# Two transformer blocks on one core: a shorter inverse root, narrower weight tiles, a finer start and moved weight splits

## The reference

```python
def rms_norm(x, g, eps):
    return x * rsqrt(mean(x * x) + eps) * g

# second block
proj = rms_norm(h, attn_pre_norm) @ w_in       # w_in: 1024 x 2072
(q_n, k_c, v_c, k_s, v_s, k_w, v_w, g_n, q_w, k_sw, v_sw) = split(proj, IN_SPLITS)
# k_sw: 2 heads x 64 = 128 columns; v_sw: 128 columns; g_n: 8 heads x 3 = 24 columns
k_c, v_c -> compress -> 15 compressed keys and values
mixed = concat([rms_norm(o_nsa), rms_norm(o_swa)]) @ w_out
h = h + rms_norm(mixed, attn_post_norm)
u = causal_dwconv(rms_norm(h, ffn_pre_norm) @ w_up)
out = h + rms_norm((gelu(gate) * up) @ w_down, ffn_post_norm)
```

## Time and profile before

| | us |
|---|---|
| three runs | 1249.72, 1247.06, 1248.22 (median 1248.22) |
| the profiled execution | 1248.38, of which the span of its instructions is 1246.5 |

### The profile page before, as it was taken

How to read it: one execution, slowest core, us unless ns; L and a number is a source line. 1 busy time by engine, 2 the same in 40 slices (tenths; PEclk the granted TensorE clock), 3 DMA queues, 4 the chain that set the end, 5 groups by cost and what they waited for, 6 DMA issues and landing times.

```text
span 1246.5 us, 24096 instructions
## 1 busy us (share of the span) xinstructions
PE 1182.5 (95%) x9150; PEld 1125.3 (90%) x9150; DVE 892.2 (72%) x1520; ACT 610.0 (49%) x1070; POOL 67.6 (5%) x56
## 2 busy tenths in 40 slices
PE   9999999999999999998999999999978898999997
PEld 8988898999999999778989999999966587999997
DVE  7999876676666587556758666556886757999854
ACT  5764644544445444344445444444455654666642
POOL 1576000000000000000000000000000000000000
PEclk9999999999999999998999999999988898999999
DMA  7453442455455556214524555556544113454563
GB/s 274 170 201 136 136 169 101 140 170 197 169 190 182 198 177 217 68 69 152 186 82 143 199 180 191 172 200 211 185 168 137 35 35 100 159 197 170 187 211 107
DMA packets 32232, 198.55 MB, mean 159 GB/s; under 512 B 3744, under 2 KB 6944, under 8 KB 9248
## 3 DMA queue, kind: packets, MB, share of 16 engines
q1 hardware_dynamic: 30240, 194.14, 45.1%
q10 hardware_dynamic: 1920, 3.41, 0.8%
HBM read 194.12 MB, written 1.05 MB: 157 GB/s over the span
## 4 chain that ended last, share of the span: by engine, by line
PE 80%; DVE 12%; ACT 4%; issue 3%; DMA 1%; DVEq 0%; ACTq 0%; SPq 0%
PE acc L495 20%; PE acc L497 20%; PE acc L496 20%; PE acc L531 7%; DVE wlo L1439 2%; PE acc L511 2%; DVE wlo L1432 2%; PE acc L778 2%; PE sc L742 1%; ACT whi L997 1%; DVE mx L1812 1%; PE tp L767 1%; DMA raw<-weights 1%; PE sc L495 1%; PE sc L496 1%
## 5 line engine op out<-in xcount | busy, mean ns | idle before, releaser
L495 PE MATMUL acc<-Hhi,whi 128*128 128x256 f32 x1376 | 391.3, 284 | 4.5 <-DVE wlo L1439 4.4
L496 PE MATMUL acc<-Hlo,whi 128*128 128x256 f32 x1376 | 389.3, 283 | 0.0
L497 PE MATMUL acc<-Hhi,wlo 128*128 128x256 f32 x1376 | 389.3, 283 | 0.0
L997 ACT ACTIVATE whi<-raw 128x1024 fp32r<-128x1024 f32 x161 | 170.0, 1056 | 329.6 <-PE acc L497 306.8
L1432 DVE TENSOR_TENSOR wlo<-raw,whi 128x1024 fp32r<-128x1024 f32 x160 | 197.1, 1232 | 107.5 <-ACT whi L997 104.7
L495 PEld LDWEIGHTS acc<-Hhi,whi 128*128 128x128 f32 x1376 | 264.1, 192 | 6.1 <-DVE wlo L1439 2.8
L496 PEld LDWEIGHTS acc<-Hlo,whi 128*128 128x128 f32 x1376 | 264.1, 192 | 0.2
L497 PEld LDWEIGHTS acc<-Hhi,wlo 128*128 128x128 f32 x1376 | 264.1, 192 | 0.0
L1439 DVE TENSOR_TENSOR wlo<-raw,whi 128x1024 fp32r<-128x1024 f32 x160 | 197.7, 1236 | 1.3
L495 PE MATMUL acc<-FH,whi 128*128 128x256 f32 x608 | 173.8, 286 | 8.3 <-DVE wlo L1439 4.5
L497 PE MATMUL acc<-FH,wlo 128*128 128x256 f32 x608 | 172.4, 284 | 0.0
(11 more groups left out here) (351 smaller groups left out, 2034.6 us busy)
## 6 DMA issues: line engine op xcount, KB each, us to landing
raw<-weights SPq DMA_DIRECT2D x177, 1024.0 KB, 4.9
MEM<-mem_in SPq DMA_DIRECT2D x2, 1024.0 KB, 7.4
held<-weights SPq DMA_DIRECT2D x2, 1024.0 KB, 5.8
E<-A ACTq DMA_DIRECT2D x14, 128.0 KB, 2.3
X<-x_in SPq DMA_DIRECT2D x4, 256.0 KB, 3.5
raw<-weights SPq DMA_DIRECT2D x2, 512.0 KB, 6.9
MEM<-consts ACTq DMA_DIRECT2D x2, 512.0 KB, 5.2
out<-MKV SPq DMA_DIRECT2D x4, 256.0 KB, 2.1
```

Source lines behind the costliest of these rows:

```text
L495: pe.matmul(dst, w, x, start=first, stop=False)
L496: pe.matmul(dst, w, xl, start=False, stop=False)
L497: return pe.matmul(dst, wl, x, start=False, stop=last)
L997: act.activation(whi[j][:, 0:HALF, :], raw[j][:, 0:HALF, :], ACT.Copy).then_inc(hi_out, 1)
```

## The change

1. **The root.** The guess is one operation (a multiply-add on the bits read as numbers), followed by one scaled step of three operations and one step of higher order of four. That is 1 + 3 + 4 operations where there were 2 + 9; with the one that adds eps, 9 instead of 12. `between` now stands after the first step.
2. **Zero columns.** `SWA_KEYS` (tile 6 of `win`) is multiplied and rotated for 128 columns, `SWA_VALUES` (`winv`) for 152; the splits of both are as narrow. The products of the left-out zero columns are not read by anything.
3. **The end of `win`.** `window_blocks(0)` runs before tile 6 is rotated, `window_rest(0)` before the split of the first `cmp` tile; PE's wait for the read of `winv`'s accumulator before the attention is gone, and in its place `hidden_part(0)` waits for the read of tile 7.
4. **The start.** X is issued by ACT's queue in another layout in memory (made on the host from the same numbers), the first weight tile comes in quarters, ACT and DVE go pair by pair, PE starts on each pair as it comes, `meanwhile` has 20 products, and PE sums all 8 chunks of squares; POOL no longer does.
5. **Attention steps.** The splits of `wout` tiles 1 and 2 move to steps 10 to 13 on ACT and 11 to 14 on DVE, `compressed` moves from step 8 to step 7.
6. **`up2`.** PE makes 14 products of `ones` into a free accumulator, which nothing reads, between `turn_x` and the wait for `MKV`.

```diff
+SWA_KEYS, SWA_VALUES = T0["win"] + 6, T0["winv"]
+WIDTHS = {SWA_KEYS: P, SWA_VALUES: P + 24}
...
-                sp.dma_start(X[:, 2 * p:2 * p + 2, :], cols(x_in)[:, 2 * p:2 * p + 2, :]).then_inc(x_loaded[p], 16)
-            sp.dma_start(raw[0][:, 0:HALF, :], tile_of(0)[:, 0:HALF, :]).then_inc(head_loaded, 16)
-            sp.dma_start(raw[0][:, HALF:KC, :], tile_of(0)[:, HALF:KC, :]).then_inc(raw_loaded[0], 16)
+                k = slice(2 * p, 2 * p + 2)
+                sp.dma_start(raw[0][:, k, :], tile_of(0)[:, k, :]).then_inc(head_loaded[p] if p < 3 else raw_loaded[0], 16)
...
-            sum_squares("mix0")
...
+                        n = slice(0, width)
+                        mm = three(dst[:, n], x[:, o], xl[:, o], w[:, n], wl[:, n], a, z)
...
+                            if name == "pw1":
+                                if p < 3:
+                                    pe.wait_ge(lo_head, p + 1)
+                                else:
+                                    tile_in(L0[name])
...
-            meanwhile(32)
+            meanwhile(20, sc[:, 3, 0:P])
...
+            tile_in(L0["win"] + 6)
+            pe.wait_ge(acc_free, G0["win"] + 7)
+            columns(0, Hhi, Hlo, 0).then_inc(tile_done, 1)
+            tile_in(L0["win"] + 7)
+            pe.wait_ge(acc_free, G0["win"] + 8)
+            for m in range(2):
+                mm = columns(1, Hhi, Hlo, m)
+            mm.then_inc(tile_done, 1)
             to_tokens("pre2")
             tile_in(L0["winv"])
             pe.wait_ge(acc_free, G0["winv"] + 1)
             for m in range(2):
-                mm = columns(0, Hhi, Hlo, m, turned=True)
+                mm = columns(0, Hhi, Hlo, m, turned=True, width=WIDTHS[SWA_VALUES])
...
+                    else:
+                        pe.wait_ge(acc_free, G0["win"] + 8 + 2)
...
-            pe.wait_ge(acc_free, G0["attn_nsa"] + 2)
...
+            pe.wait_ge(acc_free, G0["wout"] + 2 + 3)
+            meanwhile(14, acc[0][:, 0, 0:P])
...
+            for p in range(4):
+                act.dma_start(X[:, 2 * p:2 * p + 2, :], x_in[:, 2 * p * S:(2 * p + 2) * S].rearrange("p (c t) -> p c t", c=2))\
+                    .then_inc(x_loaded[p], 16)
...
+                if p < 3:
+                    act.wait_ge(head_loaded[p], 16)
+                else:
+                    act.wait_ge(raw_loaded[0], 16)
+                act.activation(pair(whi[0], 2 * p), pair(raw[0], 2 * p), ACT.Copy).then_inc(hi_out if p % 2 else hi_head, 1)
...
-                                   4: hidden_act, 6: lambda: ahead("wins", 0, 1, 0), 8: lambda: out_weight_half(2, 0),
-                                   9: lambda: out_weight_half(2, 1), 20: last_weights,
+                                   4: hidden_act, 10: lambda: out_weight_half(1, 0), 11: lambda: out_weight_half(1, 1),
+                                   12: lambda: out_weight_half(2, 0), 13: lambda: out_weight_half(2, 1), 20: last_weights,
...
-                link(dve.tensor_scalar(nwi[:, 0:n], v.bitcast(I32), 1, None, op0=ALU.logical_shift_right))
-                link(dve.tensor_scalar(y.bitcast(I32), nwi[:, 0:n], -1, 0x5F3759DF, op0=ALU.mult, op1=ALU.add))
-                for step in range(3):
-                    link(dve.scalar_tensor_tensor(out=a, in0=y, scalar=-0.5, in1=v, op0=ALU.mult, op1=ALU.mult))
-                    link(dve.tensor_tensor(out=a, in0=a, in1=y, op=ALU.mult))
-                    ins = dve.scalar_tensor_tensor(out=y if step < 2 else dst, in0=a, scalar=1.5, in1=y, op0=ALU.add, op1=ALU.mult)
-                    if step < 2:
-                        link(ins)
-                    if step == 1 and between:
-                        between()
-                return ins
...
+                link(dve.tensor_scalar(y.bitcast(I32), v.bitcast(I32), -0.5, float(0x5F1FFFF9), op0=ALU.mult, op1=ALU.add))
+                link(dve.scalar_tensor_tensor(out=a, in0=y, scalar=-GUESS_SLOPE, in1=v, op0=ALU.mult, op1=ALU.mult))
+                link(dve.tensor_tensor(out=a, in0=a, in1=y, op=ALU.mult))
+                link(dve.scalar_tensor_tensor(out=y, in0=a, scalar=GUESS_TOP, in1=y, op0=ALU.add, op1=ALU.mult))
+                if between:
+                    between()
+                link(dve.scalar_tensor_tensor(out=a, in0=y, scalar=CUBIC_SCALE, in1=v, op0=ALU.mult, op1=ALU.mult))
+                link(dve.tensor_tensor(out=a, in0=a, in1=y, op=ALU.mult))
+                link(dve.scalar_tensor_tensor(out=a, in0=a, scalar=-1.25 / CUBIC_SCALE, in1=a, op0=ALU.add, op1=ALU.mult))
+                return dve.scalar_tensor_tensor(out=dst, in0=a, scalar=1.875, in1=y, op0=ALU.add, op1=ALU.mult)
...
-            rotate("win", 6)
-            tile("win", 0, 8, 7)
-            dve.wait_ge(acc_free, G0["win"] + 7 + 2)
-            out_acc(dve.tensor_tensor(out=A[:, VC_SLOT:VC_SLOT + 2, :], in0=acc[1][:, :, :], in1=both(R[:, :]), op=ALU.mult))
...
             window_blocks(0)
+            rotate("win", 6)
+            tile("win", 0, 8, 7)
+            dve.wait_ge(acc_free, G0["win"] + 7 + 2)
+            out_acc(dve.tensor_tensor(out=A[:, VC_SLOT:VC_SLOT + 2, :], in0=acc[1][:, :, :], in1=both(R[:, :]), op=ALU.mult))
+            window_rest(0)
             ahead("win", 0, 8, 7)
             to_tokens("pre2")
             tile("winv", 0, 1, 0)
             out_acc(values_out(1, acc[0]))
-            window_rest(0)
...
-                ahead("wins", 0, 1, 0)
+                compressed()
...
-                                   5: lambda: ahead("cmp", 0, 4, 3), 6: copy_hidden, 7: step7, 8: compressed,
-                                   9: lambda: out_weight_half(2, 0), 10: lambda: out_weight_half(2, 1),
+                                   5: lambda: ahead("cmp", 0, 4, 3), 6: copy_hidden, 7: step7,
+                                   11: lambda: out_weight_half(1, 0), 12: lambda: out_weight_half(1, 1),
+                                   13: lambda: out_weight_half(2, 0), 14: lambda: out_weight_half(2, 1),
```

101 lines of the change are left out of this document (47 added, 54 removed).

## The result

The changed kernel takes 1229.28 us (median of four runs, 1227.95 to 1229.92), the kernel before 1247.64 (four runs). The ratio is 0.9845, with a 95% interval of 0.9832 to 0.9859: faster by 1.5%, 18.4 us. The profiled execution took 1229.92 with a span of 1228.1, against 1248.38 and 1246.5 before.

What follows compares the result with a forecast made beforehand. PE was taken as the bound, busy 1182.5 of 1246.5 us. Start, roots and `up2` sum to -7.35; with -1.05 (end of `win`) and -1.75 (attention) -10.15 from 1248.38, so 1238.2, said as 1238; range 1231.5 to 1242.

Steps and rivals of the forecast that it cites:

- The views and the four places: Profile readings, and where the change matters: the start, the end of `win` with the attention steps, `up2`, the tail.
- the start: Kernel start: fourth tile starts at 29.3 instead of 32.66, -3.35 us; bounds -1.6 and -4.2.
- the end of `win`: From `win`'s tile 6 to the attention's first reduction: less work and a dropped wait; -1.05 us taken, bounds -5.1 and -1.05.
- `up2`: Wait before `MKV`: dummy products keep the clock up, -2.5 us, and the root comes earlier, -0.6.
- the attention steps: Attention loop: moved splits and earlier copy shrink PE's waits; lead 2.9 less 1.1 paid in new places, -1.75 us.
- The first case: `winv`: narrow rounded products cost the 256-column time or less, shift -5.1 us, kernel 1234.2; as rival, chance 0.28.
- The second case: `winv`: narrow rounded products fall to the plain rate, 0.26 each, shift -1.05 us, kernel 1238.2; the one taken.
- The rival of splits that pay in full: Attention steps 10 to 14: four halves cost 9.1 instead of 1.1 us, 1246, or 1242 by half; chance 0.12.
- the text's lower bound: Start: only -1.6 us if transfers come a quarter later each, since DVE would then be last.
- The roots: Shorter roots: -0.6 us on the path to the output, -0.6 before `MKV`, -0.3 in the first feed-forward part.
- The feed-forward gap: First feed-forward part: the shorter root closes a DVE-made gap of under 0.4 us, -0.3.
- The slower rival: New gaps shift where the clock falls; 1.2 GHz for 31 us behind the attention costs 24.7, so 1263; chance 0.02.

Runs made afterwards that it cites:

- p_width: Changed kernel with other dummy products before `up2`: 16 each in the rounded type at 256, 200, 152, 128, 64 and 32 moving columns; 1239.7 us (one run).
- u_splits: Changed kernel with only the splits of `wout` tiles 1 and 2 at their old steps, `compressed` staying at step 7; 1235.25 us.
- u_steps: Changed kernel with part 5 alone undone: splits of `wout` tiles 1 and 2 at their old steps, `compressed` at step 8; 1235.49 us.
- x7: Changed kernel with one spare DVE operation (about 1.2 us, nothing reads it) at attention step 7; 1233.86 us.
- x12: Changed kernel with one spare DVE operation (about 1.2 us, nothing reads it) at attention step 12; 1233.49 us.
- u_root: Changed kernel with the root of before (12 operations, `between` behind its second step); 1233.78 us.
- u_dummy: Changed kernel without the 14 products of ones before `up2`; 1231.94 us.
- u_order: Changed kernel with part 3 alone undone (old order and PE's wait for the read of `winv` back), widths still narrow; 1229.53 us.

## Why the prediction was wrong, point by point

**The views and the four places** were right: the traces differ at the start, the end of `win` with the attention, `up2` and the tail, and by 0.6 us elsewhere. Two terms carry the miss of 8.2 us: the end of `win` (-1.05 forecast, -4.80 in the traces) failed in its mechanism, and the attention steps (-1.75, -7.10) in their size. With the first alone put right the forecast would have been 1234.2, still inside the range; it is the attention term that took the time below it. The start fell 1.3 us short of its forecast, which made the miss smaller by as much; that is luck.

**The width: the step whose mechanism failed.** "I take the second: every four-byte product under 256 columns that the trace shows goes at the plain rate." Those rows were all plain float32, which leaves two records for a product at any width (x8 for four products of 256 columns in the earlier trace rows as well as x38 for 19 of 128 in the earlier trace rows), while the rounded type leaves one. The price goes with the type, not with the width, and p_width shows 0.112 for every narrow width. The rows had this in them. The first case of the text, -5.1, measured -4.80. (The second case's 0.21 x 152/128 is 0.25, not 0.26, and 48 of them 12.0 us; it changes nothing.) That the formula of the Trainium skill (TensorE: Matmul & The Clock Gate, Back-to-back issue gap) pointed to the first case was right in sign, but its 66 ns was not met: 0.112 us is the spacing.

**The attention steps: the right mechanism, mis-sized.** The term was -1.75 and the traces show -7.10 from the first reduction on, -6.2 of it from step 7: 6.9 gained up to `EW`'s first transposes, 0.7 paid behind. Three parts of it went wrong. The lead was put at 2.9, without working; the two waits that the text shortens (2.22 to 0.2, 2.13 to 0.5) give 3.65. And even that reads only PE's waits of steps 7 and 8, while DVE sets the pace up to step 10, and all four halves stood on its way: two at step 7, one ahead of each of the next two waits. 4.6 of the 6.9 us come back if only the splits go back (u_splits), 7.2 with all of part 5 (u_steps), and a spare operation at step 7 costs its full length (x7). The payment in the new places was put at 1.1 (its own rows, 1.22 against 0.93 once and about 0.76 three times, give 1.7); the trace has 0.7. And the lower clock of 962.6 to 972.9, named as something that "may go", was priced at nothing: the compressed scores alone, at the higher clock, went from 3.60 to 1.96.

**The rival of splits that pay in full** did not come: the four halves, 4.9 us of DVE, cost 0.7 in their new places. The idle time before each step was the right row to read. But x12 shows that nothing is left of it at step 12.

**The start** was -3.35 and is -2.92 at the fourth tile, -2.08 at `pw2`. DVE was last there after all (0.75 of wait), as in the case of the text's lower bound (-1.6): the third tile's half on ACT began at 18.77, not at about 17.3. PE's own first product came at 7.24 and not at 8.4, which was luck: its clock rose at 4.6 us instead of the 6.9 of before (6.5 in u_root, where the first product stands at 8.07), and the wait for DVE took it back. The sentence "behind it PE has no gap until the convolution ends" failed: DVE lies beside POOL's first share for longer than before, and 0.8 us of the gain go with the wait at the seventh tile.

**The roots** were priced at 0.3 + 0.6 + 0.6 and undoing them costs 4.5 by the medians. The two small ones showed as 0.6 before `MKV` and 0.6 at the end, as said. The feed-forward gap closed twice (0.3 each), and at the fourth tile's split the root was on the path (the wait there is 2.24 in u_root, 0.75 in the changed kernel), where I had counted it inside the start. Of the 5.3 us by which u_root's trace is longer, about 1.8 are the lower clock and the slower products of `down1`, not the root's operations.

**`up2`** was right in mechanism and size (-3.1, measured -3.14), and u_dummy shows that the products do it, all but the root's 0.6.

**The order at the end of `win`** was treated together with the widths. It brings some tenths at most (u_order): one of PE's longest waits, of 4.0 us, could be put back (3.01 there) nearly for free, since what follows waits for DVE too.

**The slower rival** did not come: behind the start, the traces have 54 us at the lower clock before and 31 after.

What the undone parts cost, 4.2 + 0.3 + 6.2 + 2.4 + 4.5 + 2.7, is 20.3, near the 18.4 of the whole; each of them is uncertain by 2 to 3 us.

## What to carry to other kernels

Price a product by rows of its own type, and look at how many records one product leaves before a rate is carried over. Where several engines hand work round in steps, find which one sets the pace in each step; a piece of work moved out of such a step gains its whole length, and moved into a step where that engine idles costs little, until the idle time is used up. A long wait of PE that is followed by the lower clock costs twice. Products that nothing reads cured it at `up2`, in every trace; at `diffo` the gain is likely and not shown, and in the attention they brought none. So fill one wait at a time, and hold the trace against others without the filling before crediting it.
